# HGRN2 heads: the logarithm of the key is added to the cumulated gates, and one exponential gives key times decay

## The reference, cut to what matters

```
f = lb + (1.0 - lb) * sigmoid(hf)          # gate; the key is k = 1.0 - f
b = cumsum(log(f))                         # within a chunk
a = einsum('bthk,bshk,btshk->bhts', q, k, exp(b_t - b_s))   # s <= t
o = einsum('bhts,bshv->bthv', a, v) + einsum('bthk,bhkv->bthv', q * exp(b), s)
s = exp(b_last) * s + einsum('bshk,bshv->bhkv', k * exp(b_last - b), v)
```

## Time and profile before

| | us |
|---|---|
| median of three runs | 2138.81 |
| lowest and highest | 2136.27, 2140.71 |
| span of the profiled execution | 2134.4 |
| TensorE busy in it | 1954.5 (92%) |
| VectorE busy | 1106.8 (52%) |
| GpSimd busy | 1131.8 (53%) |
| ScalarE busy | 464.6 (22%) |

### The profile page before, as it was taken

One profiled execution on the slowest core, in us unless ns is written; L12 is line 12 of the kernel. 1 busy time (PEld: TensorE's weight loads), 2 busy tenths in 40 slices (PEclk: granted clock), 3 DMA queues, 4 the chain that ended last, 5 costly groups with the idle time before them and its releaser, 6 DMA issues.

```text
span 2134.4 us, 34113 instructions
## 1 busy us (share of the span) xinstructions
PE 1954.5 (92%) x13036; PEld 1919.0 (90%) x13036; DVE 1106.8 (52%) x1458; ACT 464.6 (22%) x671; POOL 1131.8 (53%) x644
## 2 busy tenths in 40 slices
PE   5998999998888888888888999799998999999997
PEld 4998999998777877888878999799997999999997
DVE  8776676577478889888794222600033321222123
ACT  2301010011334443444433222300012210000011
POOL 4454665557455566555664333245556455455555
PEclk8999999999899999999999999999999999999999
DMA  7342343343211111111112121022212122122222
GB/s 272 126 158 99 109 157 145 122 157 112 85 33 45 54 42 42 34 44 54 42 33 86 60 77 51 25 79 79 79 63 76 60 79 72 67 79 79 79 67 91
DMA packets 52485, 176.71 MB, mean 83 GB/s; under 512 B 6848, under 2 KB 9664, under 8 KB 52032
## 3 DMA queue, kind: packets, MB, share of 16 engines
q1 hardware_dynamic: 47952, 170.11, 22.7%
q10 hardware_dynamic: 4464, 5.64, 0.8%
HBM read 171.00 MB, written 4.72 MB: 82 GB/s over the span
## 4 chain that ended last, share of the span: by engine, by line
PE 68%; DVE 14%; issue 10%; POOL 3%; ACT 2%; DMA 1%; DVEq 1%; SPq 0%; ACTq 0%; POOLq 0%
PE acc L323 62%; DVE ada_prod L413 3%; DVE hg_qlev L786 1%; DVE hg_eb L767 1%; DVE hg_eb L768 1%; DVE hg_ef L762 1%; PE mix L933 1%; POOL hg_klev L804 1%; DVE hg_qlev L787 1%; PE mix L1223 1%; PE mix L953 1%; PE mix L966 1%; DMA ada_raw<-ada_dram 1%; POOL hg_klev L808 1%; POOL w_hi L311 1%
## 5 line engine op out<-in xcount | busy, mean ns | idle before, releaser
L311 POOL TENSOR_SCALAR w_hi<-raw 128x1024 fp32r<-128x1024 f32 x240 | 289.9, 1208 | 807.3 <-PE acc L323 706.9
L323 PE MATMUL acc<-h_hi,w_hi 128*128 128x320 f32 x2816 | 665.2, 318 | 33.2 <-DVE h_lo L517 31.8
L323 PE MATMUL acc<-h_lo,w_hi 128*128 128x320 f32 x2816 | 648.6, 312 | 0.0
L323 PE MATMUL acc<-h_hi,w_lo 128*128 128x320 f32 x2816 | 647.4, 311 | 0.0
L313 POOL TENSOR_TENSOR w_lo<-raw,w_hi 128x1024 fp32r<-128x1024 f32 x240 | 615.6, 2565 | 20.0
L323 PEld LDWEIGHTS acc<-h_hi,w_hi 128*128 128x128 f32 x2816 | 476.0, 191 | 39.6 <-issue 34.3
L323 PEld LDWEIGHTS acc<-h_lo,w_hi 128*128 128x128 f32 x2816 | 478.8, 191 | 0.0
L323 PEld LDWEIGHTS acc<-h_hi,w_lo 128*128 128x128 f32 x2816 | 476.6, 190 | 0.0
L413 DVE CUSTOM_DVE_ANT_0 ada_prod<-ada_raw,c_row 128x1024 f32<-128x1024 f32 x130 | 232.5, 1824 | 4.9 <-DMA ada_raw<-ada_dram 2.1
L528 DVE SCALAR_TENSOR_TENSOR x<-acc,mod,x 128x128 f32 x168 | 63.2, 433 | 238.6 <-PE acc L323 238.0
L323 PE MATMUL acc<-u_hi,w_hi 128*128 128x320 f32 x704 | 163.1, 313 | 13.3 <-DVE x L528 13.2
(11 more groups left out here) (215 smaller groups left out, 2028.4 us busy)
## 6 DMA issues: line engine op xcount, KB each, us to landing
raw<-w_dram SPq DMA_DIRECT2D x240, 512.0 KB, 3.7
ada_raw<-ada_dram SPq DMA_DIRECT2D x65, 512.0 KB, 5.2
ada_pe<-ada_pe_dram SPq DMA_DIRECT2D x7, 512.0 KB, 9.5
x<-x_dram SPq DMA_DIRECT2D x2, 1280.0 KB, 9.7
y_dram<-x SPq DMA_DIRECT2D x8, 320.0 KB, 2.4
c_row<-in_c_dram SPq DMA_DIRECT2D x1, 1024.0 KB, 4.5
hg_sin<-s_hg_dram ACTq DMA_DIRECT2D x8, 128.0 KB, 2.0
out_hg_dram<-hg_sfin ACTq DMA_DIRECT2D x8, 128.0 KB, 1.7
```

The lines of the kernel that those rows point to most:

```text
L311: pool.tensor_scalar(w_hi[:, slot, :], raw[:, slot, :], 1.0, 1.0, ALU.mult, ALU.mult).then_inc(hi_done, 1)
L323: last = pe.matmul(acc[g][:, b, 0:HT], w[:, s, k * P:(k + 1) * P], tile[:, b * HT:(b + 1) * HT], start=(k == 0 and n == 0), stop=(k == k_t ...
```

## The change

The key of each direction is no longer kept as k but as its logarithm, added to the cumulated gates: `k_f` becomes b_f - ln k_f and `k_b` becomes p_b + ln k_b. An argument is then a difference between the block's middle and this sum, and the exponential is already key times decay. `k_lev`, with three buffers instead of two, holds the argument and then the key; `e_q` holds the query's argument and exponential. Six things follow:

- ScalarE takes two more logarithms of 640 elements per head, of the keys, behind those of the gates. They wait for `k_sum`.
- The keys get a lower bound of 2^-62 in the instruction that scales them.
- VectorE folds the logarithms in with two instructions of 640 after the scans, and waits for them (`hg_keyed`) before the arguments of level 0.
- VectorE's two products of 320 a level become one of 640.
- `hg_keys` and its waits are gone, on GpSimd and on TensorE.
- GpSimd's order in a head is slab 1, 2, 3, 4, and the next slab 0, with nothing between.

```diff
+            act.wait_ge(hg_qk, N_QK * h + 1)
+            for k in (k_f, k_b):
+                act.activation(k[:], k[:], ACT.Ln).then_inc(hg_ln, 1)
...
-                act.activation(e_f[:, u % 2, :], e_f[:, u % 2, :], ACT.Exp)
-                act.activation(e_b[:, u % 2, :], e_b[:, u % 2, :], ACT.Exp).then_inc(hg_exp, 1)
+                act.activation(k_lev[:, u % 3, :], k_lev[:, u % 3, :], ACT.Exp)
+                act.activation(e_q[:, u % 2, :], e_q[:, u % 2, :], ACT.Exp).then_inc(hg_exp, 1)
...
-                dve.tensor_tensor(fb[:, :, 0:half], mid, src[:, :, 0:half], ALU.subtract)
-                dve.tensor_tensor(fb[:, :, half:], src[:, :, half:], mid, ALU.subtract)
...
+                dve.tensor_tensor(blocks(ka, u)[:, :, first], mid_f, blocks(k_f[:], u)[:, :, first], ALU.subtract)
+                dve.tensor_tensor(by_tile(ka)[:, :, :, second], by_tile(k_b[:])[:, :, :, second], mid_b, ALU.subtract)
+                dve.tensor_tensor(blocks(qa, u)[:, :, second], b_all[:, :, second], mid_f, ALU.subtract)
+                dve.tensor_tensor(by_tile(qa)[:, :, :, first], mid_b, p_blk[:, :, :, first],
+                                  ALU.subtract).then_inc(hg_arg, 1)
...
+            dve.tensor_tensor(q_lev[:, s, :], q[:], e_q[:, s, :], ALU.mult).then_inc(hg_qk, 1)
...
+            with pool.Fori(1, HG_HEADS) as h:
+                for p in range(1, 5):
+                    split_slab(pool, "hg", p, h)
+                split_slab(pool, "hg", 0, h + 1)
+            for p in range(1, 6):
+                split_slab(pool, "ret", p, 0)
...
-            dve.tensor_tensor(k_lev[:, 1, :], k_f[:], k_b[:], ALU.add).then_inc(hg_qk, 1)
+            dve.tensor_tensor(k_sum[:], k_f[:], k_b[:], ALU.add).then_inc(hg_qk, 1)
...
+            dve.wait_ge(hg_ln, 4 * h + 4)
+            dve.tensor_tensor(k_f[:], b_f[:], k_f[:], ALU.subtract)
+            dve.tensor_tensor(tiles5(k_b[:]), p_b[:, :, 0:P], tiles5(k_b[:]), ALU.add).then_inc(hg_keyed, 1)
+            dve.wait_ge(hg_keyed, h + 1)
...
             pe.wait_ge(hg_qk, N_QK * m + u + 1)
-            if u:
-                pe.wait_ge(hg_kk, N_ARG * m + u)
```

More of the change, by code:

```diff
@@ L766, in hg_arguments, with by_tile @@
-                mid = src[:, :, :, half:half + 1].to_broadcast([P, NT, nb, half])
-                dve.tensor_tensor(bb[:, :, :, 0:half], mid, src[:, :, :, 0:half], ALU.subtract)
-                dve.tensor_tensor(bb[:, :, :, half:], src[:, :, :, half:], mid, ALU.subtract).then_inc(hg_arg, 1)
+                first, second = slice(0, half), slice(half, 2 * half)
+                na, nb = T // (2 * half), P // (2 * half)
+                def by_tile(ap):
+                    return ap.rearrange("p (c a i) -> p c a i", c=NT, a=nb)
@@ L772, in hg_arguments @@
             else:
                 last = p_b[:, :, P:P + 1].to_broadcast([P, NT, P])
-                dve.tensor_tensor(tiles5(f), last, p_b[:, :, 0:P], ALU.subtract).then_inc(hg_arg, 1)
+                dve.tensor_tensor(tiles5(qa), last, p_all, ALU.subtract).then_inc(hg_arg, 1)
         def hg_operands(dve, m, u):
-            s, half = u % 2, 1 << u
+            s = u % 2
             dve.wait_ge(hg_exp, N_ARG * m + u + 1)
@@ L781, in hg_operands @@
                 dve.wait_ge(hg_lev, (LEVELS + 1) * m + u)
[L782 to L807, removed]
-                pool.tensor_tensor(k_lev[:, s, :], k[:], e[:, s, :], ALU.mult).then_inc(hg_kk, 1)
+            dve.tensor_tensor(q_lev[:, s, :], q[:], e_q[:, s, :], ALU.mult).then_inc(hg_qk, 1)
         def split_hg(pool):
@@ L814, in split_hg @@
             split_slab(pool, "hg", 0, 1)
-            with pool.Fori(1, HG_HEADS - 1) as h:
-                split_and_keys(pool, "hg", h, "hg", 0, h + 1)
-            split_and_keys(pool, "hg", HG_HEADS - 1, "ret", 0, 0)
-            split_and_keys(pool, "ret", HG_HEADS, "ret", 5, 0)
-        def split_and_keys(pool, name, h, next_name, next_p, next_i):
-            i = h if name == "hg" else 0
-            for p, units in ((1, (0,)), (2, (1, 2)), (3, (3, 4)), (4, (5, 6, 7, 8))):
-                split_slab(pool, name, p, i)
-                for u in units:
-                    hg_keys(pool, h - 1, u)
-            split_slab(pool, next_name, next_p, next_i)
+            with pool.Fori(1, HG_HEADS) as h:
[4 more added lines that the diff above has]
+                split_slab(pool, "ret", p, 0)
         def hg_score_read(dve, m, u):
@@ L842, in hg_start_dve @@
         def hg_start_dve(dve, h):
-            again = not (isinstance(h, int) and h == 0)
             for n, g in enumerate((g_f, g_b)):
@@ L929, in hg_unit_pe @@
             mix_free(pe, g, (Uses.hg[0] + HG0 * m + 1 + u // 2) if g == 0 else (Uses.hg[1] + HG1 * m + u // 2))
-            ks, qs = (k_lev[:, 1, :], q[:]) if u == 0 else (k_lev[:, (u - 1) % 2, :], q_lev[:, (u - 1) % 2, :])
+            ks, qs = (k_sum[:], q[:]) if u == 0 else (k_lev[:, (u - 1) % 3, :], q_lev[:, (u - 1) % 2, :])
             for c in range(NT):
```

43 lines of the change are left out of this document (19 added, 24 removed).

## The result

The changed kernel takes **2098.18 us** (median of four runs, 2095.93 to 2100.10) beside 2137.54 us for the kernel before (median of four, 2134.16 to 2140.71: one run more than the three shown ahead). The ratio is 0.9814, with a 95% interval from 0.9800 to 0.9828. The forecast was 2109.0 us, range 2086 to 2138. The gain is 39.4 us by the medians and 36.2 us by the two profiled spans (2134.4 and 2098.2); forecast were 29.8.

The account below looks back on a forecast made before the run. TensorE was taken to bound the kernel nearly everywhere, standing still often only in the eight HGRN2 heads. The terms +2.1 - 6 x 3.32 - 12.0 = -29.8 us took 2138.8 to 2109 us, range 2086 to 2138.

Parts of the forecast that it names:

- Part A: Head loop from unit 0's scores to the second key transposition: from 43.66 to 30.0 us at full clock, waits gone.
- part B: Head loop from the second key transposition to the next head's unit 0: from 22.80 to 31.2 us.
- The term for the two logarithms: ScalarE's two added key logarithms ahead of Square, on the way to the next head's unit 0: +1.35 us.
- The blocked time: GpSimd's splits of slabs 1, 2 and 3 stopping VectorE before the next unit 0: 8.3 us.
- slab 1's price: VectorE, reading the output later, meets only the end of slab 1's split in part B: 2.2 us.
- Half clock: TensorE going on at half clock after its long standstill before unit 0: 2.2 us lost per head.
- The ends: First and last heads of the HGRN2 stage: head 1's unit 0 moves +2.1 us, head 7 takes -12.0 us.
- A pass: Head loop from unit 0 to the next unit 0: 30.0 + 31.2 + 2.2 = 63.4 us, before 66.72.
- The 4.4 us: Whole kernel: the profiled span, 2134.4 us, was 4.4 below the runs' median, a difference carried into the forecast.
- Rival 1: VectorE's unbroken run holds GpSimd off, one split leaves part B: 28.1 us there, total 2091 us; chance 0.17.
- Rival 2: Late VectorE meets slab 4's split in Part A, 3.0 us wait in eight heads: 2133 us; chance 0.20.
- Rival 3: TensorE stays at half clock for 14 us after unit 0's standstill, losing 7.0 us per head: 2148 us; chance 0.11.

Follow-up runs that it names:

- e_dummy_read: `e_hold` plus 16 GpSimd products per head, sized and placed as the old key products, on an unused tile with nobody waiting; 2121.17 us, ratio 0.9922.
- e_write_long: `e_dummy_read` with its 16 GpSimd products per head exchanged for memsets that only write, 14 of them of 960 elements; 2062.96 us, ratio 0.9655.
- e_square_first: The changed kernel with ScalarE's two key logarithms moved behind Square and the next copy out of PSUM; 2093.42 us, ratio 0.9796.
- e_hold: The changed kernel with GpSimd's splits held back by waits for ScalarE's exponentials, at their places between the former key products; 2063.18 us, ratio 0.9652.
- e_hold_slab2: The changed kernel with only slab 2's split waiting, for unit 0's exponentials; slabs 3 and 4 follow freely, retention slabs not held; 2079.80 us, ratio 0.9743.

## Why the prediction was right, point by point

**Part A: right.** It was to go from 43.66 to 30.0 us plus half clock, and 29.6 plus half clock came out. There is no wait in it, and units with three k-tiles follow one another at 3.76 us (755.28 to 759.04), the step read from the earlier trace rows. VectorE's work in it, put at 25 us, is 24.09. The waits that went were more than the three that the prediction lists: the head before has two more, of 1.88 and 0.55 us at 777.96 and 781.64, and all five make up its 9.55 us of idle time. That VectorE was late mostly because it was stopped, not because it had much to do, is what `e_dummy_read` and `e_write_long` show, for 7.1 us a head; 3.7 stay open.

**The chain of part B: right in its parts, 0.7 us too long together (31.2 against 30.5).** The output read was to start 12.04 us after the transposition and starts at 11.71. The term for the two logarithms was too large: 1.35 us, where 1.02 came out. By the prediction's own figures (2 x 0.75 us from 797.0 on, against 797.08) it would even be 1.4. But the first of them begins 0.22 us after the end of the gates' logarithms, and from each to the next instruction it is 0.64 us:

```profile
783.20 0.74 ACT L707 ACTIVATE hg_kf<-hg_kf 128x640 f32<-128x640 f32 x1 [0.22 <-DVE hg_ksum L829]
...
784.47 0.69 ACT L742 ACTIVATE hg_osquare<-mix 128x640 f32<-128x640 f32 x1
```

Square starts 10.83 us after the transposition, and started 9.79 after it before. The blocked time was put at 8.3 us (2.2 + 3.06 + 3.06) and is 8.2. From L882 to the first subtraction the forecast has 5.29 + 1.76 + 8.3 = 15.35 us, and the trace 14.98; the wait for the folded keys costs 0.13 us, not the 0.3 taken from the earlier trace rows. From there to unit 0 it is 3.85 instead of 3.76. The Ln term and slab 1's price must be read together: 1.35 us later, but 0.86 less of the split, 0.5 net. `e_square_first` has 0.3.

**Half clock: right on average, not in each pass, and partly by luck.** 2.2 us were taken, between the 1.5 and the 3 of two unlike rows. The wait is the same to 0.1 us in each of the six passes, and the loss is 1.5 us in some and 2.9 in others; 2.2 is their mean. The prediction's row for it was one after a wait of 10.36 us. Here TensorE at 741.07 shows 2.50 us for ten matmuls that take 1.28 at full clock, and the part has a granted clock of 0.90.

**The ends: right.** Unit 1 of head 0 was forecast at 620.5 and is at 621.47, head 1's unit 0 at 679.0 and is at 679.36. Head 7 gains 12.4 instead of 12.0 us.

**Where the size was off.** The term is "A pass is then 30.0 + 31.2 + 2.2 = 63.4 us": it measured 62.3 (62.31 in the mean of six). 0.4 us of the difference lie in part A, whose terms add up to 29.6 and were made 30.0 "with a few tenths between them", which weren't needed. 0.7 lie in part B: 0.3 in the two logarithms, 0.2 in the folding (1.52 instead of 1.76) and 0.15 in the blocked time. Small as this is, it counts six times: the six passes gave 26.2 us and not 19.9, and that is the whole gap between 29.8 and the 36.2 us of the spans. The remaining 3 us up to the 39.4 of the medians are scatter: the span of the profiled execution before lies 3.1 us under the median of four, that of the changed kernel, whose execution is the slowest of its four (2100.10 us), lies at the median. The 4.4 us that the prediction carried along from span to median were those of one execution, and not there after; the time of one execution is 1.8 to 1.9 us above its span in all four runs of the changed kernel.

**Rival 1**, that VectorE's chain holds GpSimd off in part B, did not happen. No w_lo of the six passes takes more than 3.06 us. The one at 786.40 that is longer than its free 2.4 was held up by a single instruction, the output gate at 786.36. The Trainium skill ("SBUF — State Buffer", section "SBUF: two separate sides") has it that whoever starts first keeps the pair of SBUF ports that the two engines share for the whole instruction. The scans agree: at each change between w_hi and w_lo one of them gets in, and the next waits for the whole of GpSimd's instruction, as the one at 787.10 with its 2.63 us. But the mechanism of rival 1 is real, only not at the scans. In `e_hold`, w_hi takes 3.0 to 3.2 us instead of 1.04 twelve times in the stage. Each time it starts 0.1 to 0.3 us behind the first subtraction of a level and ends only 0.9 us behind the level's product, the fifth instruction of an unbroken run:

```profile
795.63 3.03 POOL L311 TENSOR_SCALAR w_hi<-raw 128x1024 fp32r<-128x1024 f32 x1 [2.91 <-ACT hg_eq L718]
...
795.32 0.48 DVE L771 TENSOR_TENSOR hg_klev<-hg_bf,hg_kf 128x320 f32<-128x320 f32 x1
...
796.92 0.82 DVE L789 TENSOR_TENSOR hg_qlev<-hg_q,hg_eq 128x640 f32<-128x640 f32 x1
```

These rows, like the one at 766.82, don't agree with that rule, by which GpSimd would get in behind one instruction, and the measurement decides. Yet the w_hi at 804.15 of the same run, 0.3 us behind the same subtraction, takes 1.06 us. What decides who gets in, no run shows.

**Rival 2**, a remaining wait in part A, did not happen in the changed kernel. Slab 4's split does fall in part A, at 751.88, but no unit waits behind it. Slabs 2's and 3's splits had moved out into part B (GpSimd is busy for 4.89 us in part A). Where they were moved back, the waits came: part A is 34.8 us in two passes of `e_hold` and 34.5 on average in `e_hold_slab2`. The mechanism was real; the one split that the rival names was not enough for it.

**Rival 3**, the clock, did not happen. The mean granted clock of the whole execution is 0.962, against 0.965 before. (Its price adds up to 2147 us, not to the 2148 given: 2109 + 8 x 4.8.)

**What the prediction didn't draw out** is that the change is two changes. Taking the key products away frees VectorE in part A. Taking away the waits which came with them sets slabs 2 and 3 free, and these collide with the scans, for 5.9 us of part B in each pass. The prediction saw that collision and priced it right (2 x 3.06), but took it as given, and did not ask what the change would be worth with the pace kept: 35 us more.

## What to carry to other kernels

When work is taken off an engine, look at what its waits were pacing, and keep the pace if it was useful: here waits in front of the prefetch splits were worth 35.0 us beside the 39.4 of the change itself, and a single one of them, ahead of slab 2's split, 18.4. Price VectorE's standstill beside GpSimd by the length of the neighbour's instructions that read SBUF beside it, not by the neighbour's busy share. And an edit ahead of such a collision is worth only what the collision doesn't take back: 1.1 us earlier gave 0.3 in part B.

## What the runs showed of the hardware

A GpSimd instruction that only writes left VectorE alone. 14 memsets of 0.90 us and two longer ones per head cost nothing (2062.96 us beside 2063.18), while 16 products in the same places cost 58 us (2121.17). VectorE's subtraction of 320 took 0.48 us beside a memset, 1.00 us beside a product, 1.32 us beside w_hi and 2.70 us beside w_lo. The Trainium skill ("SBUF — State Buffer", section "SBUF: two separate sides") says that an operation of VectorE with two SBUF inputs is in conflict "only against a GpSimd op that reads SBUF"; these runs agree.

Not every standstill is of the full length: three splits with 11.1 us of rows stopped the scans for 8.2. Nor is it always VectorE that is stopped: w_hi took 3.03 us instead of 1.04 behind an unbroken run of VectorE's (`e_hold`, 795.63). And the loss after the same wait of 8.3 us was 1.5 us in one pass and 2.9 in the next, so that a single half-clock episode of a trace is no good measure of the mean.
